# Handing the key lookups of two gathered tiles from VectorE to GpSimd, in a two-layer hybrid diffusion step

## What is computed

```python
q = (x @ lp['peer_wq']).reshape(t, PEER_HEADS, 2, PEER_HALF)
sc = jnp.einsum('thpd,hpnd->thpn', q, lp['peer_subkeys'])
sv, si = lax.top_k(sc, PEER_TOPK)                       # 16 of 128 keys, twice per head
cand = (sv[:, :, 0, :, None] + sv[:, :, 1, None, :]).reshape(t, 8, 256)
cidx = (si[:, :, 0, :, None] * 128 + si[:, :, 1, None, :]).reshape(t, 8, 256)
top_v, top_p = lax.top_k(cand, PEER_TOPK)
experts = jnp.take_along_axis(cidx, top_p, axis=-1)     # 8 heads x 16 experts per token
gates = jax.nn.softmax(top_v, axis=-1)
```

## Time and profile before

| | |
|---|---|
| median of three runs | 4597.29 us |
| the profiled execution, its own time | 4596.96 us |
| its span in the trace | 4595.2 us |
| VectorE busy | 3414.1 us (74%), 6080 instructions |
| TensorE busy (matmuls) | 4070.1 us (89%) |
| ScalarE busy | 1590.4 us (35%) |
| GpSimd busy | 1930.9 us (42%), 1099 instructions |

### The profile page before, as it was taken

The page is one execution under the profiler, slowest core; times in us unless marked ns, Lnnn a source line. Parts: engine busy times, 40 slices in busy tenths (PEclk is TensorE's granted clock), DMA queues, the critical chain, the costliest instruction groups (busy, mean ns, idle before and its releaser), DMA issues.

```text
span 4595.2 us, 67474 instructions
## 1 busy us (share of the span) xinstructions
PE 4070.1 (89%) x23702; PEld 3569.7 (78%) x23702; DVE 3414.1 (74%) x6080; ACT 1590.4 (35%) x2615; POOL 1930.9 (42%) x1099
## 2 busy tenths in 40 slices
PE   6889999864899999999888899997558999999996
PEld 5866789754798988988777678897447989889885
DVE  2407336889799999999953173468897999999998
ACT  2226322256433333333232362222563333333331
POOL 1200220000487777877622003100006877788774
PEclk9999999987999999999989899999889999999998
DMA  5220564532899999999843107644339999999996
GB/s 223 102 107 10 193 234 177 204 110 83 313 400 395 395 396 369 404 392 390 327 198 141 66 1 253 224 184 156 110 111 369 404 391 392 395 376 401 391 389 249
DMA packets 343859, 1197.47 MB, mean 261 GB/s; under 512 B 27392, under 2 KB 125744, under 8 KB 278128
## 3 DMA queue, kind: packets, MB, share of 16 engines
q1 hardware_dynamic: 89072, 561.55, 31.5%
q0 software_dynamic: 151168, 552.73, 30.9%
q10 hardware_dynamic: 103424, 80.74, 5.3%
HBM read 1085.08 MB, written 109.84 MB: 260 GB/s over the span
## 4 chain that ended last, share of the span: by engine, by line
DVE 33%; PE 30%; POOL 12%; DVEq 9%; issue 9%; DMA 5%; ACT 2%; ACTq 0%; SPq 0%; POOLq 0%
PE PS L781 9%; POOL got_a L756 6%; DVE acc L2317 6%; POOL got_b L756 6%; DVE ring_lo L2287 5%; PE PS L790 5%; PE PS L791 4%; PE PS L792 4%; DVEq L2309 3%; DVE spare L2317 3%; DVEq L2294 3%; PE PS L785 2%; DMA ring<-weights 2%; PE PS L954 2%; DMA got_a<-u_rows,sidx 2%
## 5 line engine op out<-in xcount | busy, mean ns | idle before, releaser
L756 POOL DMA_INDIRECT got_a<-u_rows,sidx x256 | 442.6, 1729 | 1156.6 <-DMA gate_matrix<-stg 1062.8
L1601 ACT CAST ring_hi<-ring 128x2048 fp32r<-128x2048 f32 x256 | 489.6, 1913 | 1265.7 <-DMA ring<-weights 1265.7
L790 PE MATMUL PS<-hT_hi,ring_hi 128*128 128x384 f32 x2048 | 687.4, 336 | 20.0 <-DVE ring_lo L2287 20.0
L792 PE MATMUL PS<-hT_hi,ring_lo 128*128 128x384 f32 x2048 | 687.1, 335 | 0.0
L791 PE MATMUL PS<-hT_lo,ring_hi 128*128 128x384 f32 x2048 | 686.4, 335 | 0.0
L790 PE MATMUL PS<-ring_hi,W_hi 128*128 128x512 f32 x1536 | 609.7, 397 | 54.5 <-DVE W_lo L2303 54.4
L791 PE MATMUL PS<-ring_lo,W_hi 128*128 128x512 f32 x1536 | 606.9, 395 | 0.0
L792 PE MATMUL PS<-ring_hi,W_lo 128*128 128x512 f32 x1536 | 606.6, 395 | 0.0
L2287 DVE TENSOR_TENSOR ring_lo<-ring,ring_hi 128x2048 fp32r<-128x2048 f32 x256 | 585.1, 2286 | 4.2 <-ACT ring_hi L1601 4.2
L756 POOL DMA_INDIRECT got_b<-u_rows,sidx x256 | 435.5, 1701 | 135.8 <-issue 66.4
L756 POOL DMA_INDIRECT got_b<-v_rows,sidx x256 | 416.7, 1628 | 160.0 <-DVE acc L2317 85.5
(11 more groups left out here) (369 smaller groups left out, 8501.2 us busy)
## 6 DMA issues: line engine op xcount, KB each, us to landing
ring<-weights SPq DMA_DIRECT2D x412, 1024.0 KB, 7.8
G<-gate_matrix SPq DMA_DIRECT2D x128, 384.0 KB, 9.2
gate_matrix<-stg ACTq DMA_DIRECT2D x10, 4096.0 KB, 15.9
gate_splits<-mhi ACTq DMA_DIRECT2D x24, 1024.0 KB, 10.2
gate_splits<-ring_lo SPq DMA_DIRECT2D x24, 1024.0 KB, 10.1
ring_lo<-gate_splits SPq DMA_DIRECT2D x24, 1024.0 KB, 7.2
mhi<-gate_splits SPq DMA_DIRECT2D x24, 1024.0 KB, 4.9
gate_matrix<-stg ACTq DMA_DIRECT2D x2, 3584.0 KB, 22.0
```

The lines of the kernel that those rows point to most:

```text
L756: pool.indirect_dma_start(out=got[n % GB], out_offset=None, in_=u_rows[:, :] if phase % 2 == 0 else v_rows[:, :], in_offset=bass.IndirectO ...
L790: mm(out, a_hi, b_hi, start=first, stop=False)
L792: return mm(out, a_lo, b_hi, start=False, stop=final)
L1601: nc.scalar.copy(ring_hi[s][:, :], ring[:, s, :]).then_inc(hi_ready, 1)
```

## The change

For tiles 0 and 1, VectorE keeps the comparison (`spots_of`, step 9) and the gates (`gates_of`, step 10). GpSimd takes the product, the three sums and the last sum into `idx_a` (`keys_of`), once VectorE's mask and ScalarE's `sif16` are there. VectorE makes the row numbers of tile 0 behind step 4 of tile 1 (piece 12), those of tile 1 behind the last lower half of the merge. Tiles 2 to 4 stay as they were.

```diff
+                def keys_of(t):
+                    c = cand16_a
+                    add = nc.gpsimd.tensor_tensor
+                    pool.wait_ge(spots_ready, layer_at(l, NS, t + 1))
+                    pool.wait_ge(sif16_ready, layer_at(l, NT, t + 1))
+                    add(c[:, :, :, :], c[:, :, :, :], sif16_a[:, :, :, :], ALU.mult)
+                    pool.drain()
+                    for n in (8, 4, 2):
+                        add(c[:, :, 0:n, :], c[:, :, 0:n, :], c[:, :, n:2 * n, :], ALU.add)
+                        pool.drain()
+                    add(idx_a[:, 0:2, :].rearrange("p a (h k) -> p a h k", k=TOPK),
+                        c[:, :, 0, :].rearrange("p (a h) k -> p a h k", a=2), c[:, :, 1, :].rearrange("p (a h) k -> p a h k", a=2),
+                        ALU.add).then_inc(keys_found, 1)
+
+                for t in range(NS):
+                    keys_of(t)
...
+                def spots_of(t, b):
+                    spots = b.pif[:, :, :].rearrange("p a (h k) -> p (a h) k", k=TOPK)
+                    tt(b.cand16[:, :, :, :], steps[:, :, :].unsqueeze(1).broadcast_to([P, 16, TOPK, TOPK]),
+                       spots.unsqueeze(2).broadcast_to([P, 16, TOPK, TOPK]), ALU.is_equal).then_inc(spots_ready, 1)
...
                 def listed(t):
-                    chosen(t, set_a, sgate[:, t, :])
+                    dve.wait_ge(keys_found, layer_at(l, NS, t + 1))
...
                     if step == 4:
                         found_next(b)
+                        if t == 1:
+                            listed(0)
...
-                    if step == 9:
+                    if step == 9 and t < NS:
+                        spots_of(t, b)
+                    elif step == 9:
                         looked_up(t, b)
                     if step == 10:
-                        listed(t)
+                        gates_of(t, b, sgate[:, t, :])
+                        dve.drain()
...
                 merged_lo(1, 6)
                 merged_lo(1, 7)
+                listed(1)
```

More of the change, by code:

```diff
@@ L493, in trunk @@
         exp_ready = sem("exp_ready")
+        spots_ready = sem("spots_ready")
+        keys_found = sem("keys_found")
         idx_ready = sem("idx_ready")
@@ L2154, in looked_up, with gates_of @@
                     dve.drain()
+                def spots_of(t, b):
+                    spots = b.pif[:, :, :].rearrange("p a (h k) -> p (a h) k", k=TOPK)
+                    tt(b.cand16[:, :, :, :], steps[:, :, :].unsqueeze(1).broadcast_to([P, 16, TOPK, TOPK]),
+                       spots.unsqueeze(2).broadcast_to([P, 16, TOPK, TOPK]), ALU.is_equal).then_inc(spots_ready, 1)
+                def gates_of(t, b, gates):
+                    dve.wait_ge(exp_ready, l * NT + t + 1)
+                    reduce(b.pm[:, 0:8], b.pw[:, :, :], AX.X, ALU.add)
+                    dve.drain()
+                    nc.vector.reciprocal(b.pm[:, 8:16], b.pm[:, 0:8])
+                    dve.drain()
+                    return tt(gates.rearrange("p (h k) -> p h k", h=8), b.pw[:, :, :],
+                              b.pm[:, 8:16].unsqueeze(2).broadcast_to([P, 8, TOPK]), ALU.mult)
                 def chosen(t, b, gates):
@@ L2163, in chosen @@
                     dve.drain()
[L2164 to L2170, removed]
+                    return gates_of(t, b, gates)
                 def listed(t):
-                    chosen(t, set_a, sgate[:, t, :])
+                    dve.wait_ge(keys_found, layer_at(l, NS, t + 1))
                     ts_(idx_a[:, 0, :], idx_a[:, 0, :], float(KEYS), const[:, bass.ds(l + C_BASE, 1)], ALU.mult, ALU.add)
```

## The result

The changed kernel takes 4609.07 us (median of 8 runs, 4607.62 to 4614.12), the kernel before 4597.04 us beside it (8 runs): ratio 1.0029, with 95% confidence 1.0018 to 1.0040. It is 12.0 us slower. The forecast was 30.8 us slower: the right side, and the time lies inside the range, but the change is only 0.4 of the forecast one.

What follows compares the result with a forecast made beforehand. In the second group's merge TensorE bounds for most of its length, VectorE near its end. 2 layers x (6.6 + 8.8) = 30.8 us on the profiled 4596.96 us gave 4628 us, 0.67% slower; range 4600 to 4650.

Steps and rivals of the forecast that it cites:

- The mechanism: In the second group's merge, VectorE operations on two SBUF inputs stand still until GpSimd's current instruction ends.
- Term 2: Tile 1, from piece 17's sum to the first lower half: held sums delay the output projection by 8.8 us per layer.
- term 1: Tile 0, from the gate product to piece 15: held operations and moved row numbers delay TensorE by 6.6 us per layer.
- I take the element's price: GpSimd's 16-bit operations cost 2.2 ns an element, as its f32 subtraction: product 9.1 us, sums 4.6, 2.3, 1.15, 0.6.
- GpSimd's first sum then holds: Tile 0: GpSimd's first sum holds VectorE until 803.0 us, so piece 8's sum ends 5.9 us late.
- passes whole: Tile 0's delay of 6.6 us is not caught up at piece 14 and reaches piece 15 in full.
- by the same amount: The output projection and everything behind it are late by the full delay, 6.6 plus 8.8 us per layer.
- The clock: TensorE idles up to 6 us at a time and its clock may fall; counted as nothing, 3 us in the range.
- The byte's price: Rival: GpSimd's 16-bit operations cost half, product 4.6 us; some 1.3 us lost per layer, 4600 us; chance 8%.
- No holding up: Rival: GpSimd does not hold VectorE with these operands; TensorE's 3.8 us wait per layer is saved, 4589.5 us; chance 6%.
- Dearer GpSimd: Rival: GpSimd costs 1.5 times the element's price, 4659 us; chance 12% together with held products from PSUM.
- held products from PSUM: Rival: a piece's first product, PSUM and SBUF inputs, is held too, 4642 us; chance 12% together with dearer GpSimd.

Runs made afterwards that it cites:

- early drain: The changed kernel with one more GpSimd drain just before its wait for tile 0's row of places; median 4618.57 us, ratio 1.0036 to the kernel before.
- tile 0 alone: The changed kernel with only tile 0's lookup on GpSimd, tile 1's back on VectorE; median 4598.04 us, ratio 1.0004 to the kernel before.
- the two kernels that gain on the kernel before: The changed kernel with gates made before the comparison, tile 0's row numbers moved, GpSimd's instructions cut to 512 or 256 elements; 4594.14 and 4587.82 us.
- the two kernels whose gathers all fetch one row: The changed kernel with GpSimd's lookup replaced by one memset of the indices, or by memsets of its large tile and the indices; 4637.01 and 4640.57 us.

## Why the prediction was half right

**The mechanism held; three terms that it was turned into did not.** VectorE's operations on two SBUF inputs stand still until GpSimd's instruction ends, those that read PSUM go on, the gate product takes 5.25 and 3.35 us (forecast about 6 and 4), piece 17's sum 7.75 (about 9), and nothing waited for the keys. Piece 8's sum, forecast at 4 us or more, takes 0.43. Of the 21.7 us taken off VectorE 8.0 come through where nothing is held, and the holds cost more than that.

The miss is 30.8 - 12.0 = 18.8 us, and falls into three parts:

**GpSimd's price in both terms: 8.4 us.** With the gap out of the way (early drain) the stretches grow 22.4 us, not 30.8. Term 2 measured 6.3 us (changed kernel less tile 0 alone), where I had 8.8; term 1 148.7 - 143.7 = 5.0, where I had 6.6. The step that failed is "I take the element's price" from the subtraction in f32: 2.2 ns an element, where the bf16 product takes 7.95 / 4096 = 1.94 ns. It goes by the element and not by the byte, but an eighth cheaper (a tenth at equal size: 4.08 us for the first sum, 4.56 for the subtraction). To this came 0.3 to 0.5 us that my timeline left between GpSimd's instructions, where 0.14 us is measured. My estimate from the Trainium skill's GPSIMD Engine Reference (3.1), 8.9 us for the product, was nearer than 9.1 and also too high, against 7.95 measured.

**Term 1's step "GpSimd's first sum then holds": 5.0 us.** It assumed that the sum follows the product at once, as nothing in the trace of before had GpSimd draining. The first drain of a layer costs 1.2 or 8.2 us more, and piece 8's sum slipped through the gap. What was left of term 1 in layer 0 is 0.8 us from the gate product's hold and 0.8 from the moved row numbers: 1.6 for 6.6. In layer 1 the late first sums hold piece 10's instead (2.06 for 0.43): 3.2. The early drain gives the 5.0 us back, and piece 8's sum with them: it ends 4.1 us later in the stretch than before, the row numbers add 0.8, and the 4.9 us stay up to piece 16. So the step that the delay "passes whole" held. (5.9 and 0.8 are 6.7, not 6.6; this changes nothing.)

**Outside the stretch: 5.4 us, cause open.** The stretches grew 17.4 us, the median 12.0. The step that failed is that all behind the projection is late "by the same amount". In the two profiled executions the outside is 5.9 us shorter: 8.3 us come from the parts between a layer's first gather and its end (1117.25 us before, 1113.94 in the changed kernel; layer 1 1151.01 and 1146.07), and 3.1 us are lost again between the layers, where executions scatter by more than that. What it is not: a repayment of the delay, since the two kernels that gain on the kernel before have it too; and not the drains. I had argued only about the path to the projection, and nothing about the gathers but that they are not late.

**The clock.** Rows of windows of the changed kernel (length; busy PE, PEld, DVE, ACT, POOL; granted clock; DMA share; GB/s):

```profile
852.00:856.00 4.00, 3.63 (x17) 3.63 (x18) 3.76 (x4) 0.40 (x1) 3.86 (x2) 0.50 0.00 0
```

```profile
850.00:860.00 10.00, 7.63 (x34) 7.32 (x35) 9.38 (x7) 0.43 (x2) 9.43 (x5) 0.66 0.04 18
```

The same 10 us had 1.00 before. Behind TensorE's wait of 4.15 us the granted clock is 0.50, the lower level of 1.2 GHz: the matmuls start 0.21 us apart, and 0.12 us apart from 860 us on, at 2.4 GHz. I had counted nothing for the clock because VectorE binds there, and in the stretch it cost nothing. The first lower half, the last operation that is held, ends 7.90 us later in the stretch than before (119.68 against 111.78 us), and the whole stretch is 7.91 us longer; in layer 1 it is 9.50 and 9.51.

**The rivals.** The byte's price is refuted (7.95 us for the product, not 4.6). "No holding up" too; but its price of 3.8 us a layer was right in size, since the run without GpSimd's work has 4.0. Dearer GpSimd and held products from PSUM are both refuted by the rows above.

## What to carry to other kernels

Before moving work to GpSimd, ask which VectorE operations with both inputs in SBUF will fall beside it, and how long the single GpSimd instruction is: a held operation pays up to one whole instruction. The same work in pieces of 256 elements, with the gates first and tile 0's row numbers moved, turned +12 us into -11 us. Changing the order alone only passed the hold on to another operation, at 0.6 to 0.7 us more. Place small moved work where its engine already waits; that was worth 0.8 us a layer here. Ask, too, whether the freed work was late at all: tile 0's was not. Bound a forecast by whether the new instructions really follow each other; a first drain can put a gap there which changes what is hit.

## What the runs showed of the hardware

- A drain on GpSimd is cheap (0.14 us), but the first in a layer costs 1.23 us in layer 0 and 8.25 us in layer 1, to 0.05 us the same in every kernel here that has one. It does so behind a product, behind a memset (1.20 and 8.23), and behind the subtraction, in the kernel before too (1.2 and 8.2). Why, and why layer 1's is longer, stays open.
- GpSimd's price at 16 bits goes about by the element: 7.95, 4.08, 2.13, 1.15 and 0.67 us for 4096, 2048, 1024, 512 and 256 elements per partition with two inputs. Its memset of 4096 bf16 takes 3.51 us.
- GpSimd's memset of 3.51 us held up none of VectorE's operations (0.29 and 0.43 us as alone); its product and sums held those on two SBUF inputs (7.75 us for 0.43) until the single instruction ended, and not those with an input in PSUM (0.42 us).
- In the two kernels whose gathers all fetch one row, the part from the first gather on took 26 to 30 us more in layer 0 and 20 to 21 us more in layer 1 than before.
